# A two-block sequence model in fp32: each weight tile rounded, subtracted and waited for in two halves

## What is computed

```python
def swiglu(h, w_gate, w_up, w_down):
    return (jax.nn.silu(h @ w_gate) * (h @ w_up)) @ w_down

def moe_swiglu(h, w_router, w_gate, w_up, w_down):
    ...
    for e in range(N_EXPERTS):
        y = swiglu(h, w_gate[e], w_up[e], w_down[e])
        out = out + gates[..., e:e + 1].astype(h.dtype) * y
    return out
```

## Time and profile before

| | before |
|---|---|
| median of 3 runs | 2333.78 us (2333.63 to 2339.19) |
| the profiled execution, its own time | 2334.28 us |
| its span in the trace | 2332.5 us |
| PE busy | 2198.6 us, 94% |
| DVE busy | 1625.0 us, 70% |
| ACT busy | 1371.8 us, 59% |
| loads | 538.11 MB, 231 GB/s over the span |
| mean granted clock of TensorE | 0.975 of full speed |

### The profile page before, as it was taken

How to read it: one execution, slowest core, us unless ns; L and a number is a source line. 1 busy time by engine, 2 the same in 40 slices (tenths; PEclk the granted TensorE clock), 3 DMA queues, 4 the chain that set the end, 5 groups by cost and what they waited for, 6 DMA issues and landing times.

```text
span 2332.5 us, 28046 instructions
## 1 busy us (share of the span) xinstructions
PE 2198.6 (94%) x10098; PEld 1767.0 (76%) x10099; DVE 1625.0 (70%) x1882; ACT 1371.8 (59%) x1501; POOL 25.9 (1%) x28
## 2 busy tenths in 40 slices
PE   7889999789999999999999999989999899999987
PEld 6668887567878787878878787868778677778776
DVE  4554456548888888888888888876656665555664
ACT  5444446446677676767677676765445554445563
POOL 0000000000000000000000000000110000020000
PEclk9989999889999999999999999999999899999999
DMA  7235554049979897989889798945433244433323
GB/s 298 101 108 182 192 182 150 36 174 333 366 309 365 305 365 312 362 330 342 341 330 367 309 364 307 363 190 200 161 145 135 101 163 151 177 142 144 127 109 108
DMA packets 77585, 539.18 MB, mean 231 GB/s; under 512 B 10672, under 2 KB 10928, under 8 KB 12352
## 3 DMA queue, kind: packets, MB, share of 16 engines
q1 hardware_dynamic: 77504, 538.11, 61.4%
HBM read 537.02 MB, written 1.05 MB: 231 GB/s over the span
## 4 chain that ended last, share of the span: by engine, by line
PE 87%; DVE 5%; ACT 5%; issue 3%; DMA 0%; SPq 0%; ACTq 0%; DVEq 0%
PE bank L199 26%; PE bank L201 25%; PE bank L200 25%; PE bank L705 4%; ACT w_high L174 2%; DVE w_low L179 2%; PE bank L1414 1%; PE bank L1439 1%; PE bank L1975 1%; PE bank L1974 1%; ACT hy_sc L2231 0%; DMA ring<-in_gla_in_tiles 0%; DVE hy_sc L2272 0%; PE bank L2019 0%; PE bank L2020 0%
## 5 line engine op out<-in xcount | busy, mean ns | idle before, releaser
L179 DVE TENSOR_TENSOR w_low<-ring,w_high 128x2048 fp32r<-128x2048 f32 x235 | 538.2, 2295 | 313.0 <-ACT w_high L174 313.0
L174 ACT ACTIVATE w_high<-ring 128x2048 fp32r<-128x2048 f32 x235 | 448.6, 1914 | 245.6 <-PE bank L201 215.1
L199 PE MATMUL bank<-w_high,xT_high 128*128 128x512 f32 x1072 | 432.0, 403 | 26.3 <-DVE w_low L179 16.7
L200 PE MATMUL bank<-w_low,xT_high 128*128 128x512 f32 x1072 | 422.3, 394 | 0.0
L201 PE MATMUL bank<-w_high,xT_low 128*128 128x512 f32 x1072 | 422.0, 394 | 0.0
L199 PE MATMUL bank<-w_high,moe_x_high 128*128 128x512 f32 x896 | 366.7, 409 | 6.5 <-DVE w_low L179 4.4
L179 DVE TENSOR_TENSOR w_low<-moe_ring,w_high 128x2048 fp32r<-128x2048 f32 x144 | 330.0, 2291 | 49.3 <-ACT w_high L174 49.3
L201 PE MATMUL bank<-w_high,moe_x_low 128*128 128x512 f32 x896 | 354.3, 395 | 0.0
L200 PE MATMUL bank<-w_low,moe_x_high 128*128 128x512 f32 x896 | 352.9, 394 | 0.0
L179 DVE TENSOR_TENSOR w_low<-ring_wide,w_high 128x2048 fp32r<-128x2048 f32 x129 | 295.7, 2292 | 78.7 <-ACT w_high L174 78.6
L174 ACT ACTIVATE w_high<-moe_ring 128x2048 fp32r<-128x2048 f32 x144 | 275.5, 1913 | 25.8 <-PE bank L201 25.8
(11 more groups left out here) (337 smaller groups left out, 2400.5 us busy)
## 6 DMA issues: line engine op xcount, KB each, us to landing
moe_ring<-in_moe_tiles SPq DMA_DIRECT2D x144, 1024.0 KB, 4.8
ring<-in_hy_tiles SPq DMA_DIRECT2D x104, 1024.0 KB, 4.8
ring<-in_moe_tiles SPq DMA_DIRECT2D x98, 1024.0 KB, 4.8
ring_wide<-in_moe_tiles SPq DMA_DIRECT2D x97, 1024.0 KB, 4.8
ring<-in_ffn_tiles SPq DMA_DIRECT2D x17, 1024.0 KB, 4.8
ring_wide<-in_ffn_tiles SPq DMA_DIRECT2D x16, 1024.0 KB, 4.8
ring<-in_gla_in_tiles SPq DMA_DIRECT2D x6, 1024.0 KB, 7.7
ring_wide<-in_gla_in_tiles SPq DMA_DIRECT2D x6, 1024.0 KB, 11.2
```

Source lines behind the costliest of these rows:

```text
L174: self.nc.scalar.activation(self.high[:, place, :], memory, ACT.Copy).then_inc(self.rounded, 1)
L179: self.nc.vector.tensor_tensor(self.low[:, place, :], memory, self.high[:, place, :].bitcast(F32), ALU.subtract).then_inc(self.split, 1)
L199: nc.tensor.matmul(out, x[0], w[0], start=start, stop=False, **more)
L200: nc.tensor.matmul(out, x[0], w[1], start=False, stop=False, **more)
```

## The change

The rounding and the subtraction of a tile are each made of two instructions over 128x1024, with a semaphore of their own for the first half (`rounded_first`, `split_first`); the old ones are incremented by the second half. PE waits for `split_first` ahead of a tile's first matmul and for `split` ahead of the first matmul of its second half. In `block_half` both waits stand in the pass for t = 0 only. ACT's waits for the load and for `used` stand ahead of the first half, the slot of the ring is freed by the second as before. In the linear attention eight of the stage's own semaphores give way to shared ones of the kernel, counted on with `close`; who waits for what stays.

```diff
--- before.py
+++ after.py
@@ -49,6 +49,7 @@
 
 SLOT = 4 * 512
 SPLIT = 3
+FIRST, SECOND = slice(0, SLOT // 2), slice(SLOT // 2, SLOT)
 RING, RING_WIDE = 2, 4
 MOE_RING = 7
 
@@ -120,6 +121,8 @@
         self.nc, self.ctx, self.prefix, self.high, self.low = nc, ctx, prefix, high, low
         self.rounded = ctx.enter_context(nc.semaphore(prefix + "rounded"))
         self.split = ctx.enter_context(nc.semaphore(prefix + "split"))
+        self.rounded_first = ctx.enter_context(nc.semaphore(prefix + "rounded_first"))
+        self.split_first = ctx.enter_context(nc.semaphore(prefix + "split_first"))
         self.used = ctx.enter_context(nc.semaphore(prefix + "used"))
         self.landing = {}
         self.landed = {}
@@ -171,12 +174,17 @@
         act.wait_ge(landed, value)
         if before is not None:
             act.wait_ge(self.used, before)
-        self.nc.scalar.activation(self.high[:, place, :], memory, ACT.Copy).then_inc(self.rounded, 1)
+        self.nc.scalar.activation(self.high[:, place, FIRST], memory[:, FIRST], ACT.Copy).then_inc(self.rounded_first, 1)
+        self.nc.scalar.activation(self.high[:, place, SECOND], memory[:, SECOND], ACT.Copy).then_inc(self.rounded, 1)
 
     def rest_of_tile(self, dve, place, memory, rounded):
 
+        dve.wait_ge(self.rounded_first, rounded)
+        self.nc.vector.tensor_tensor(self.low[:, place, FIRST], memory[:, FIRST], self.high[:, place, FIRST].bitcast(F32),
+                                     ALU.subtract).then_inc(self.split_first, 1)
         dve.wait_ge(self.rounded, rounded)
-        self.nc.vector.tensor_tensor(self.low[:, place, :], memory, self.high[:, place, :].bitcast(F32), ALU.subtract).then_inc(self.split, 1)
+        self.nc.vector.tensor_tensor(self.low[:, place, SECOND], memory[:, SECOND], self.high[:, place, SECOND].bitcast(F32),
+                                     ALU.subtract).then_inc(self.split, 1)
 
     def prepare(self, eng, who, upto):
 
@@ -616,7 +624,6 @@
             wait_all(pe, lhs_ready)
             for v, (j, half) in enumerate(order):
                 tile = first + v
-                pe.wait_ge(W.split, tile + 1)
                 for t, evac in enumerate((K.evac_act, K.evac_dve)):
                     if j >= 2 and half == 0:
                         pe.wait_ge(evac.sem, evac.at(j - 1))
@@ -624,7 +631,7 @@
                         if half == 0 and (j, t) != (0, 0):
                             pe.wait_ge(*head.ready(1, j))
                         head.operand(pe, half, t, target(j))
-                    last = block_half(nc, K.bank[(2 * j + t) % 4], lhs[j], W, tile % SPLIT, t, half)
+                    last = block_half(nc, K.bank[(2 * j + t) % 4], lhs[j], W, tile % SPLIT, t, half, pe, tile + 1)
                     if t == 1:
                         last.then_inc(W.used, 1)
                     elif half == 1:
@@ -690,9 +697,11 @@
     return lambda n, t: ((K.evac_dve if t else K.evac_act).sem, base[t] + n + 1)
 
 
-def block_half(nc, bank, lhs, W, place, t, half):
+def block_half(nc, bank, lhs, W, place, t, half, pe, number):
 
     for k in range(4):
+        if t == 0 and k % 2 == 0:
+            pe.wait_ge(W.split if k else W.split_first, number)
         kk = 4 * half + k
         last = matmul3(nc, bank[:], tuple(x[:, kk, t * P:(t + 1) * P] for x in lhs), W.operand(place, slice(k * 512, (k + 1) * 512)),
                        start=(kk == 0), stop=(kk == KC - 1))
...
@@ -801,17 +810,17 @@
                 for evac in (K.evac_act, K.evac_dve):
                     pe.wait_ge(evac.sem, evac.at(beside.n))
                 for t, bank in ((0, 4), (1, 7)):
-                    transposes(nc, K, B[bank], [ke[:, hd, t * P:(t + 1) * P] for hd in range(GLA_H)]).then_inc(ev["keT"], 1)
-
-                pe.wait_ge(ev["kend"], ev.at("kend", 2))
+                    transposes(nc, K, B[bank], [ke[:, hd, t * P:(t + 1) * P] for hd in range(GLA_H)]).then_inc(ev["turned"], 1)
+
+                pe.wait_ge(ev["pT"], ev.at("pT", 2))
                 for n, banks in ((0, (0, 1)), (1, (2, 3)), (2, (4, 7))):
...
@@ -1010,13 +1019,12 @@
             def _(pe):
                 def gate_up(c, half):
                     tile = number["guB" if half else "guA", c]
-                    pe.wait_ge(W.split, tile + 1)
                     for t in range(TT):
                         if c == 0:
                             head.operand(pe, half, t)
                         elif half == 0:
                             pe.wait_ge(s_hid, 2 * (c - 1) + t + 1)
-                        last = block_half(nc, B[4 + t], K.xT, W, tile % SPLIT, t, half)
+                        last = block_half(nc, B[4 + t], K.xT, W, tile % SPLIT, t, half, pe, tile + 1)
                         if t == 1:
                             last.then_inc(W.used, 1)
                         elif half:
@@ -1030,10 +1038,11 @@
 
                 def down(c, groups, last_group):
                     tile = number["dn", c]
-                    pe.wait_ge(W.split, tile + 1)
                     pe.wait_ge(s_hT, c + 1)
                     for n, t in groups:
                         for f in range(2):
+                            if (n, t) == (0, 0):
+                                pe.wait_ge(W.split if f else W.split_first, tile + 1)
                             last = matmul3(nc, B[2 * t + n][:], tuple(x[:, c % 2, f, t * P:(t + 1) * P] for x in hT),
                                            W.operand(tile % SPLIT, slice(f * D + n * 512, f * D + (n + 1) * 512)),
                                            start=(c == 0 and f == 0), stop=(c == N - 1 and f == 1))
@@ -1459,13 +1468,14 @@
 
             def gate_up(c, half):
                 at = G.first + number["guB" if half else "guA", c]
-                pe.wait_ge(F.split, n * PER + (at + 1))
                 if half == 0 and c == 0:
                     pe.wait_ge(G.xg, 2 * n + 2)
                 elif half == 0 and c >= 2:
                     pe.wait_ge(G.hid, n * N + c - 1)
                 for k in range(4):
                     kk = 4 * half + k
+                    if k % 2 == 0:
+                        pe.wait_ge(F.split if k else F.split_first, n * PER + (at + 1))
                     last = matmul3(nc, B[4 + c % 2][:], (xg[0][:, kk, :], xg[1][:, kk, :]), F.operand(at % SPLIT, slice(k * 512, (k + 1) * 512)),
                                    start=(kk == 0), stop=(kk == KC - 1))
                 last.then_inc(F.used, 1)
@@ -1476,9 +1486,9 @@
 
             def down(c):
                 at = G.first + number["dn", c]
-                pe.wait_ge(F.split, n * PER + (at + 1))
                 pe.wait_ge(G.hT, n * N + c + 1)
                 for f in range(2):
+                    pe.wait_ge(F.split if f else F.split_first, n * PER + (at + 1))
                     for half in range(2):
                         last = matmul3(nc, B[half][:], tuple(x[:, c % 2, f * P:(f + 1) * P] for x in hT),
                                        F.operand(at % SPLIT, slice(f * D + half * 512, f * D + (half + 1) * 512)),
```

More of the change, by code:

```diff
@@ L757, in gla @@
         quad = lambda b: b[:].rearrange("p (h s) -> p h s", h=4)
-        ev = Sems(K, ("w_lr_high", "w_lr_low", "diag", "rows_psum", "rows", "lr", "lrT", "gate", "z", "ln", "b", "exp", "end", "endexp", "qk_turned", "qd", "keT", "kend", "score", "aT", "kv", "state", "silu",
-                      "values", "squared", "head_var", "head_std", "yb", "ogT", "product", "oT_high", "oT_low", "chain_b", "chain"))
+        ev = Sems(K, ("w_lr_high", "w_lr_low", "diag", "rows_psum", "rows", "lr", "lrT", "sigmoid", "z", "ln", "b", "exp", "end", "endexp", "qk_turned", "qd", "turned", "pT", "score", "masked", "values_out", "state", "silu",
+                      "values", "squared", "head_var", "head_std", "yb", "ogT", "product", "oT_high", "merged", "chain_b", "chain"))
         beside = Beside(K, K.t_gla[4:], lambda j, t: r[:, t, 512 * j:512 * (j + 1)], (B[4], B[7]))
@@ L788, in _ @@
                     last = nc.tensor.matmul(pair(B[5 + hd // 2])[:, hd % 2, :], w_up[:, hd * P:(hd + 1) * P], lrT[:], start=True, stop=True)
-                last.then_inc(ev["gate"], 1)
+                last.then_inc(ev["sigmoid"], 1)
                 for tile in range(2 * beside.n):
@@ L1838, in pe @@
         K, W, j, half = self.K, self.K.W, v // 2, v % 2
-        pe.wait_ge(W.split, self.first + v + 1)
         for t, evac in enumerate((K.evac_act, K.evac_dve)):
@@ L1842, in pe @@
                 pe.wait_ge(evac.sem, evac.at(j))
-            last = block_half(K.nc, self.banks[t], self.lhs[j], W, (self.first + v) % SPLIT, t, half)
+            last = block_half(K.nc, self.banks[t], self.lhs[j], W, (self.first + v) % SPLIT, t, half, pe, self.first + v + 1)
             if t == 1:
@@ L2340, in tile @@
                     n = first + number[u]
-                    pe.wait_ge(W.split, n + 1)
                     for t in range(TT):
```

22 lines of the change are left out of this document (11 added, 11 removed).

## The result

| | before | after |
|---|---|---|
| median | 2333.7 us (2332.86 to 2339.19, 4 runs) | 2310.07 us (2308.45 to 2310.51, 4 runs) |
| after / before | | 0.9893, 95% interval 0.9875 to 0.991 |
| profiled execution, its span | 2332.5 us | 2307.9 us |
| mean granted clock | 0.975 | 0.978 |

The change saves 23.6 us by the medians, 24.6 us by the two spans. A second timing in another stretch of chip time gave 2310.17 and a ratio of 0.9894 (0.9876 to 0.9912), so this is a firm number. Two executions of the study, one of the kernel before (3686.51 us) and one of the second timing (3677.21 us), ran at a granted clock of 0.555 and are left out of all ratios; without it the second timing's median is 2309.66.

What follows compares the result with a forecast made beforehand. TensorE (PE), busy 94% of the span, was taken as the bound, so only its stalls could be won. Eight points gave 21.3 us, the clock 2.1; 23.4 off the median 2333.78 gave 2310.4, range 2303 to 2322.

Steps and rivals of the forecast that it cites:

- 1 start: Kernel start: PE's first product waits for the first tile and would come 1.9 us earlier.
- 2 seven borders: Borders between experts: PE's 0.8 us stall for the next expert's first tile goes in seven places, 5.5 us.
- 3 end of experts, first hybrid tile: Behind the experts: copy of `y` for PE's scatter 0.7 us earlier, first hybrid tile 1.06 earlier; together 1.8.
- 4 stick-breaking: PE's waits for `sb_kT` and twice `sb_xq_low`, each behind a subtraction that waited for ACT: 3 x 0.8 = 2.4 us.
- 5 and 6 attention of the hybrid layers: Second attention: `hy_negmax`, `hy_pc` stalls shrink 0.9 each, 3.6 us; first attention and its end: `hy_u`, `xn` waits go, 2.4.
- 7 projections, stalls: Hybrid projections: PE's waits for `hy_u` twice a layer and `h` once shrink, 5 x 0.8 = 4.0 us.
- 7 clock behind `h`: First hybrid layer: with 0.8 us less idle before `h`, the clock behind it stays up, 2.1 us more.
- 8 losses: Subtractions that had not waited, ahead of routing and `xT_low`, and ACT's second half in stick-breaking: -0.3 us.
- The clock gives more: Rival: shortened `hy_negmax` stalls keep the clock, so matmuls behind them run faster; 2307.6 us, chance 0.25.
- Only the tile waits pay: Rival: gains behind the subtraction are taken back by waits for PE's use of older tiles; 2321 us, chance 0.13.
- It does nothing: Rival: the second semaphore holds PE at a tile's start, or the second half is always late; 2330 us, chance 0.04.
- DVE becomes the bound: Rival: two half subtractions cost over 0.35 us more a tile, so DVE bounds the expert step; 2365 us, chance 0.03.

Runs made afterwards that it cites:

- E1: The change, but PE waits for a tile's second half at its start, as before; 2313.25 us, ratio 0.9902 to the kernel before.
- E12: The change itself run once more, nothing altered; 2310.17 us, ratio 0.9894 to the kernel before.
- E7: The change, but with whole tiles in the overflow stage, which is branched over with this data; 2309.55 us, ratio 0.989 to the kernel before.
- E2: The change, but DVE starts its first half only when ACT has rounded both; 2333.77 us, ratio 0.9993 to the kernel before.
- E5: The change with quarters of 128x512 instead of halves, PE waiting for each; 2317.03 us, ratio 0.9923 to the kernel before.
- E11: The kernel before, whole tiles, with DVE's tile work behind the next mask and the weights in the second attention; 2317.78 us, ratio 0.9925.
- E9: The change, with DVE's tile work behind the next mask and the weights in the second attention; 2299.95 us, ratio 0.9852 to the kernel before.
- E4: The change, but whole tiles in the expert stage and halves only outside it; 2317.03 us, ratio 0.9924 to the kernel before.

## Why the prediction was right

Forecast 2310.4, measured 2310.07. The mechanism held: the stalls that the prediction named shrank or went, nearly all by the sizes it gave. That the total came within 0.4 us is luck. Three terms were too small, by 4.0 us together, and three too large, by 3.2, and the two ways of measuring, medians and spans, differ by 1 us themselves. The gain of each stretch is the distance of the same two PE instructions before and after:

| step | predicted | measured |
|---|---|---|
| 1 start | 1.9 | 2.4 |
| 2 seven borders | 5.5 | 8.1 |
| 3 end of experts, first hybrid tile | 0.7 + 1.06 | 0.7 + 0.5 |
| 4 stick-breaking | 2.4 | 3.3 |
| 5 and 6 attention of the hybrid layers | 3.6 + 2.4 | 3.9 |
| 7 projections, stalls | 4.0 | 4.0 |
| 7 clock behind `h` | 2.1 | 1.6 |
| 8 losses | -0.3 | -0.35 in the routing |

Small stretches beside these (-0.3 in the first layer, +0.3 and +0.4 around the experts) bring it to 24.6 by the spans.

1. **Start.** 1.83 from the halves (4.29 to 2.46), and 0.53 because the first rounding began earlier, at 11.06. The second part isn't the change's: the load's landing differs from run to run, and E1 began at 10.66, E12, the change itself, at 11.81.
2. **Borders: mis-sized.** The stall of 0.80 went, in all seven. But an expert became 1.16 shorter. The rest is 0.10 for the second matmul behind a stall (0.33 apart from the first instead of 0.23), and 0.23 at a place inside each expert where PE had been held for `moe_hiddenT_low`, which stood in DVE's queue behind a subtraction (before, the product at 810.35 came 0.39 after the one ahead of it and the next one 0.30 after that, where 0.23 is usual). The prediction had put the inside of an expert at nothing, since "all nine waits of PE for `w_low` are accounted for"; this wait is for another result, and one shorter than a matmul's modelled end isn't in the list of waits at all.
3. **End of experts: half right.** `moe_y` came 0.7 earlier. From the scatter to the first hybrid tile only 0.5 was won: 1.3 from the scatter's clock (8 matmuls in 5.37 instead of 6.66) and 1.0 from the half subtraction, less 1.75 of DVE's longer idle time behind the loop (E7). Neither the first nor the last was in the sum.
4. **Stick-breaking: the clock left out.** The three stalls shrank by 1.07, 0.79 and 0.79, 2.65 together. The rest, 0.6, is the clock, for which the sum had no term here: over the eight microseconds behind the third stall it is 0.79 (before 0.58, won about 1.1), behind the second 0.57 (before 0.63, lost about 0.5).
5. **Hybrid attention: mechanism right, return overlooked.** The stalls shrank by 0.87 and 1.09 in each layer, beside 0.9 predicted, and those of point 6 went. But the short stall behind `hy_negmax` grew from 0.82 to 1.17 and 1.29 (from start to start, less a product's own time), and 1.0 and 0.6 us were given back behind `hy_pc`: the granted clock there is 0.69 and 0.74 where it was 0.81 and 0.82. The fall to 1.2 GHz came later in the shorter stall, 1.8 us ahead of its end in the first layer and before 3.8 (in the 7.3 us up to the end the clock is 0.88, before 0.74), and so more of the slow time fell on work. What the sum put at nothing behind these stalls was thus a loss of some 2.4 us, and it is the largest of the terms that were too large.
6. **Projections.** Four waits for `hy_u` 0.8 shorter, `h` 0.77: right, and the first layer's end kept its clock, also as predicted:

```profile
1928.42 0.66 PE L714 MATMUL bank<-consts_sb,h 128*128 128x128 f32 x4 [1.49 <-DVE h L2483]
```

1.49 idle instead of 2.27, and the 1.00 of the stretch above behind it.

**The rivals.** *The clock gives more* fell: behind 2.14 us of idle for `hy_negmax` the clock was lost, in the first layer for as much as before (0.57 over eight microseconds, before 0.62), in the second for less (0.79, before 0.64). The Trainium skill (TensorE: Matmul & The Clock Gate, Part 1: The HAM clock gate) says that an idle PE falls to half rate; the trace agrees, with 0.60 in the 5 us behind. *Only the tile waits pay* is refuted by the table: points 4 to 7 brought 12.8 us, where it had 4. *It does nothing* describes E2, where DVE's first wait is on the second half's semaphore. *DVE becomes the bound* did not happen even with quarters: E5's steady step is still 8.59 with DVE busy for 8.21 of it, and what E5 lost stands behind DVE's idle time at the turn of the loop. By the Trainium skill's fixed cost (Perfetto Trace Analysis, Optimizing Scalar/DVE Operations) the 508 more subtractions would be 30 us, an estimate; the page of the profile shows 43 in all, near the 45 by the rows. The prediction read that section as speaking against the split. It also says that breaking up instructions may let work end sooner where the two engines are not saturated but cause idle time on others, and with DVE busy for 70% of the span before and 72% after, the run agrees with that sentence.

## What to carry to other kernels

When one engine prepares an operand and a second refines it, splitting the job so that the two overlap can be worth more to whatever stands behind it in the second engine's queue than to the consumer of the operand. By the table some 15 of the 24 us came that way (`moe_y`, the wait inside each expert, points 4 to 7), and some 9 at PE's waits for a tile. Nearly all of the gain needed the overlap of ACT and DVE (without it 1.6 us were left), and 2 us PE's early start. Before splitting, look at the order of that queue: moving the job behind two results that PE wants sooner was worth 17.5 us without one instruction more, and then the split paid only elsewhere. Before splitting finer, look for new idle time of the engine and not only at its busy share: the quarters that helped outside the experts cost more than they won inside the loop, behind 3.5 us in which DVE did nothing. One semaphore that counts parts serves every grain.

## What the hardware showed unexpectedly

- **Equal idle, other clock.** PE idle for 2.29 us in E11 had a granted clock of 1.00 behind it, for 2.27 us before `h` (before) 0.76, for 2.36 in E9 0.81. The length of one idle time doesn't decide; shortening it from 5.9 to 4.8 even made the work behind it slower. The scatter behind the experts took 6.66, 5.37 and, in E4, 3.67 us for the same eight matmuls, after 3.40, 2.68 and 3.40 of idle.
- **A first instruction behind a loop, or at its turn,** waited for nothing that the list of waits shows: DVE 3.3 to 5.1 us behind the loop over the experts, and 3.3 to 3.5 us at every turn of it in E5, whose code on DVE is the longest. Each of these waits ended 1.6 to 1.8 us after a DMA packet of the kind "instruction". That points to the loading of code, which no run varied alone.
